# Differential attention: key and value projections of the next head issued in two runs of 12 matmuls, spread over all eight slots

## What is computed

```python
def diff_mixer(h, cos, sin, layer_idx, w_qkv, lam_q1, lam_k1, lam_q2, lam_k2, w_o):
    q, k, v = jnp.split(h @ w_qkv, [DIFF_QK_WIDTH, 2 * DIFF_QK_WIDTH], axis=-1)
    ...
    q = jnp.concatenate([apply_rope(q[..., :DIFF_ROPE], cos, sin), q[..., DIFF_ROPE:]], axis=-1)
    k = jnp.concatenate([apply_rope(k[..., :DIFF_ROPE], cos, sin), k[..., DIFF_ROPE:]], axis=-1)
    ...
        sc = jnp.einsum('bqhcd,bkhcd->bhcqk', qb, k).astype(f32) * scale
        p = jax.nn.softmax(sc, axis=-1)
        a = (p[:, :, 0] - lam * p[:, :, 1]).astype(v.dtype)
        return jnp.einsum('bhqk,bkhe->bqhe', a, v)
```

## Time and profile before

| | us |
|---|---|
| median of 3 runs | 3125.02 |
| lowest, highest | 3124.98, 3127.79 |
| span of the profiled execution | 3121.7 |
| TensorE busy in it | 2930.5 |
| VectorE busy | 1643.0 |
| ScalarE busy | 1230.4 |
| GpSimd busy | 1077.3 |

### The profile page before, as it was taken

One profiled execution on the slowest core, in us unless ns is written; L12 is line 12 of the kernel. 1 busy time (PEld: TensorE's weight loads), 2 busy tenths in 40 slices (PEclk: granted clock), 3 DMA queues, 4 the chain that ended last, 5 costly groups with the idle time before them and its releaser, 6 DMA issues. The chain is left out here.

```text
span 3121.7 us, 39393 instructions
## 1 busy us (share of the span) xinstructions
PE 2930.5 (94%) x14436; PEld 2442.1 (78%) x14436; DVE 1643.0 (53%) x2222; ACT 1230.4 (39%) x1830; POOL 1077.3 (35%) x807
## 2 busy tenths in 40 slices
PE   6799999999899999999978999998798999999997
PEld 5688888887688888888757887877777888888885
DVE  6477777773443333433457777777534333433335
ACT  4467666662322222212245565555313222212221
POOL 3333444332332233322244444443223233222330
PEclk9999999999999999999989999999899999999998
DMA  3000000002111111111020000000311111111111
GB/s 110 22 10 9 13 8 8 8 15 101 48 54 41 41 56 58 47 40 41 27 96 24 32 28 28 28 25 24 128 41 54 41 63 52 47 40 40 40 54 54
DMA packets 35816, 132.46 MB, mean 42 GB/s; under 512 B 4480, under 2 KB 4736, under 8 KB 35328
## 3 DMA queue, kind: packets, MB, share of 16 engines
q1 hardware_dynamic: 35712, 131.03, 12.0%
HBM read 117.38 MB, written 13.63 MB: 42 GB/s over the span
## 5 line engine op out<-in xcount | busy, mean ns | idle before, releaser
L320 POOL TENSOR_TENSOR weights_lo<-weights_raw,weights_hi 128x1024 fp32r<-128x1024 f32 (+1 forms) x150 | 356.7, 2378 | 1101.5 <-ACT weights_hi L315 1101.5
L329 PE MATMUL ffn_pre<-hh,weights_hi 128*128 128x512 f32 x1408 | 558.0, 396 | 11.0 <-POOL hl L170 9.4
L331 PE MATMUL ffn_pre<-hh,weights_lo 128*128 128x512 f32 x1408 | 556.9, 395 | 0.0
L330 PE MATMUL ffn_pre<-hl,weights_hi 128*128 128x512 f32 x1408 | 556.8, 395 | 0.0
L700 DVE SCALAR_TENSOR_TENSOR ffn_conv<-ffn_pre,vecs,ffn_conv 128x1023 f32<-128x1023 f32 x88 | 112.9, 1283 | 708.0 <-ACT ffn_conv L629 708.0
L629 ACT ACTIVATE ffn_conv<-ffn_pre,vecs 128x1024 f32<-128x1024 f32 x88 | 106.3, 1208 | 819.1 <-PE ffn_pre L331 819.1
L329 PEld LDWEIGHTS ffn_pre<-hh,weights_hi 128*128 128x128 f32 x1408 | 266.0, 189 | 77.5 <-issue 12.0
L331 PEld LDWEIGHTS ffn_pre<-hh,weights_lo 128*128 128x128 f32 x1408 | 266.1, 189 | 62.3
L330 PEld LDWEIGHTS ffn_pre<-hl,weights_hi 128*128 128x128 f32 x1408 | 266.1, 189 | 61.6
L329 PE MATMUL ffn_acc<-ffn_yh,ffn_dn_hi 128*128 128x512 f32 x704 | 275.6, 391 | 12.5 <-POOL ffn_dn_lo L320 12.5
L330 PE MATMUL ffn_acc<-ffn_yl,ffn_dn_hi 128*128 128x512 f32 x704 | 275.3, 391 | 0.0
(11 more groups left out here) (248 smaller groups left out, 6266.4 us busy)
## 6 DMA issues: line engine op xcount, KB each, us to landing
weights_raw<-in_up SPq DMA_DIRECT2D x88, 512.0 KB, 3.7
ffn_dn_raw<-in_down SPq DMA_DIRECT2D x44, 512.0 KB, 3.6
weights_raw<-in_diff_qkv SPq DMA_DIRECT2D x24, 512.0 KB, 3.7
weights_raw<-in_mla_heads SPq DMA_DIRECT2D x16, 320.0 KB, 2.8
heads<-in_x SPq DMA_DIRECT2D x8, 512.0 KB, 7.0
weights_raw<-in_mla_o SPq DMA_DIRECT2D x8, 512.0 KB, 3.9
x_first<-in_x SPq DMA_DIRECT2D x1, 4096.0 KB, 12.1
x_spill<-x_first SPq DMA_DIRECT2D x1, 4096.0 KB, 13.5
```

The costliest lines, as they stand in the source:

```text
L320: pool.tensor_tensor(w.lo[:], w.raw[:], w.hi[:].bitcast(F32), ALU.subtract).then_inc(w.lo_done, 1)
L329: pe.matmul(out, w_hi, x_hi, start=start, stop=False)
L330: pe.matmul(out, w_hi, x_lo, start=False, stop=False)
L331: return pe.matmul(out, w_lo, x_hi, start=False, stop=stop)
```

## The change

The number of instructions stays; their order within the queues of four engines changes.

- TensorE: `project` takes a range of its eight k-tiles. `begin` issues the first four (12 matmuls; it waits for the weight and for the bank), `complete` the last four (it signals `proj_ready`). K0 begins at t = 1 and is completed at t = 2, K1 at 2 and 3, V0 at 5 and 6, V1 at 6 and 7; a completion stands right behind the scores of its slot. At t = 3 the values come ahead of `turn_v(TURN0)`.
- ScalarE: K0, K1, V0 and V1 are taken at t = 2, 3, 6 and 7, right behind the exponentials.
- GpSimd: the cosine products of K0 and K1 move from t = 1 and 2 to t = 2 and 3, at t = 2 behind `low_q(Q1)`.
- VectorE: at t = 2 and 3 the shuffle comes behind the reciprocal; `low_v(TURN1)` moves from t = 4 to the end of t = 3.

```diff
@@ ScalarE, slot
+                if scores and more and t in (2, 3, 6, 7):
+                    take(h + 1, {2: K0, 3: K1, 6: V0, 7: V1}[t])
                 if t % 2 == 1 and not (first and t < LAG_V):
...
                     if t == 1:
                         split_high(act, wq, h + 1, bank(h, Q1) + 1)
-                        take(h + 1, K0)
-                    if t == 2:
-                        take(h + 1, K1)
...
-                    if t == 5:
-                        take(h + 1, V0)
                     if t == 6:
                         high_parts(h + 1, 1 - parity, Q0)
-                        take(h + 1, V1)
@@ GpSimd, slot
                     if t == 1:
                         split_low(pool, wq, h + 1)
+                    if t == 2:
                         by_cosine(h + 1, K0)
-                    if t == 2:
+                    if t == 3:
                         by_cosine(h + 1, K1)
-                    if t == 3:
                         split_low(pool, wkv, 2 * h + 3)
@@ VectorE, slot
-                    if turning:
+                    if turning and t not in (2, 3):
                         shuffle(*turning)
-                    if t == 4:
-                        low_v(h, TURN1)
-                        if more:
-                            rotate(h + 1, K1)
+                    if more and t == 4:
+                        rotate(h + 1, K1)
                     col = 2 * (t % 2)
                     dve.wait_ge(exp_done, 2 * n + 2)
                     dve.reciprocal(inv_sum[:, col:col + 2], row_sum[:, col:col + 2]).then_inc(inv_ready, 1)
+                    if turning and t in (2, 3):
+                        shuffle(*turning)
                     if t == 3:
                         low_v(h, TURN0)
...
+                if t == 3:
+                    low_v(h, TURN1)
                 if turning and t != 3:
                     rotate(*turning)
@@ TensorE
-            def project(h, use, w, content):
+            def project(h, use, w, content, rows=range(KT)):
...
-                wait_weight(pe, w, content)
-                need(pe, proj_taken, bank(h, use))
-                for k in range(KT):
+                if rows[0] == 0:
+                    wait_weight(pe, w, content)
+                    need(pe, proj_taken, bank(h, use))
+                for k in rows:
...
-                mm.then_inc(proj_ready, 1)
+                if rows[-1] == KT - 1:
+                    mm.then_inc(proj_ready, 1)
+
+            def begin(h, use, w, content):
+                project(h, use, w, content, range(KT // 2))
+
+            def complete(h, use, w, content):
+                project(h, use, w, content, range(KT // 2, KT))
...
+                if scores and more and t in (2, 3):
+                    complete(h + 1, K0 if t == 2 else K1, wkv, 2 * h + 2)
+                if scores and more and t in (6, 7):
+                    complete(h + 1, V0 if t == 6 else V1, wkv, 2 * h + 3)
+                if t % 2 == 1 and not (first and t < LAG_V):
+                    values(h, t)
                 if scores and t == 3:
                     turn_v(h, TURN0)
-                if t % 2 == 1 and not (first and t < LAG_V):
-                    values(h, t)
...
                     if t in (1, 2):
-                        project(h + 1, K0 if t == 1 else K1, wkv, 2 * h + 2)
+                        begin(h + 1, K0 if t == 1 else K1, wkv, 2 * h + 2)
...
                     if t in (5, 6):
-                        project(h + 1, V0 if t == 5 else V1, wkv, 2 * h + 3)
+                        begin(h + 1, V0 if t == 5 else V1, wkv, 2 * h + 3)
```

## The result

| | median, us | profiled execution, us |
|---|---|---|
| kernel before, same session | 3125.0 | 3121.7 |
| changed kernel | 3181.8 (3175.6 to 3183.7) | 3173.4 |

The ratio is 1.0178, with a 95% interval of 1.0163 to 1.0192: slower by 56.8 us. The forecast was 3190, within 3165 to 3212.

What follows compares the result with a forecast made beforehand. TensorE sets the pace, with a four-engine loop per slot close behind. A head: 9.0 - 1.3 + 1.85 = +9.6 us; seven heads 67, less 2, total +65, so the median becomes 3190, range 3165 to 3212.

Steps and rivals of the forecast that it cites:

- Step 2: Slot 2: K1's second half waits for ScalarE's copy of K0, late behind both exponentials; 2.3 us lost a head.
- Step 3: Slots 2 and 3: K0's cosine product behind low_q delays rotation, mix and maxima; TensorE waits 6.1 us before TURN0 every head.
- Item 4: Slots 2 and 3: VectorE's one-column add and shuffle, now behind the reciprocal, held by GpSimd's scaling; 1.2 us, bounds 0 and 2.5.
- the -2 below: Correction over all heads: old TURN waits swallowed by the new wait, first head lacking values; -2 us, between -6 and +2.
- Item 5: Slot 3: lower clock after the 6.1 us wait slows TURN0 and T(3); 0.3 us on the chain, 0 to 0.8.
- Step 7: Slots 5 to 7: late mix for slot 6 delays V1's first half; S(5) to next S(0) 27.15, today 25.30: +1.85 us.
- step 1: TensorE's slots by itself; T(0) keeps its wait for the mix, only S(0) lying between T(7) and T(0); cost 0.
- The rival "faster": No exponential late, projection halves run on arrival, waits of 1.52 and 1.70 go: 28 us, so 3097; chance 0.02.
- The rival at 3140: The rotation's wait does not bite, low_q being done before K0's product is wanted; +2 a head; chance 0.07.

Runs made afterwards that it cites:

- e5: e1 with GpSimd's split of wq in slot 1 waiting until VectorE has finished Q1's rotation; 3124.7 us, ratio 1.0004 to the kernel before.
- e1: Changed kernel with GpSimd's cosine product of K0 moved ahead of low_q in slot 2; 3139.8 us, ratio 1.0047 to the kernel before.
- e2: Changed kernel with VectorE's rotation of K0 moved behind the maxima of slot 3, GpSimd's order kept; 3141.1 us, ratio 1.0046 to the kernel before.
- e8: e7 with V1's second half behind the transposes of slot 7 and ScalarE's copy of V1 at that slot's end; 3101.4 us, ratio 0.9930.
- e7: e5 with VectorE's low part of K1 moved from the end of slot 5 to the end of slot 6; 3113.5 us, ratio 0.9969.
- e10: Kernel before, whole projections, with the edits of e5 and e7; 3146.7 us, ratio 1.0074.

## Why the prediction was right

Its sign and mechanism held, and most terms are within a few tenths. Counted from S(1) = 1791.93:

- Step 2. Mix for slot 2 at 10.67 (10.66 forecast), K1 at 16.03 (16.1), S(3) at 18.94 (18.95). Shown by e5.
- Step 3. low_q starts at 19.45 (19.55), its end and the product 0.1 and more earlier: product 25.1 to 26.4 (25.2 to 26.5), mix 27.02 (27.15), TURN0 32.39 (32.65), TensorE's wait 5.77 (6.1; 5.3 in the mean of seven heads). e1 and e2 show that this queue is three quarters of the loss.
- Item 4 was mis-sized: 1.2 us a head forecast, none measured. In slot 2 the one-column add was indeed held (0.95), off the path; in slot 3, started 0.07 after the scaling had begun, it took 0.19. The row from which I took the price was an add of 512 columns beside a long split. Seven times 1.2 is 8.4 us, and the forecast was too high by as much (3190 for 3182), but that is chance: the next items take a part of it back, and the -2 below was too small.
- Item 5. TURN0 to its high part took 1.16 and to TURN1 2.62 in all, where 2.02 is the figure at the higher level: 0.6 more and not 0.3. From TURN1 to S(4) it took 0.71 where 0.41 was counted, so that the clock cost 0.9 on this chain, above the stated 0 to 0.8. The granted clock of the 15 us around it was 0.78, and 0.50, the level of 1.2 GHz, from 1824.0 to 1829.5, behind the wait of 5.8.
- S(4) came at 35.72 (36.55), Q0 3.91 after it (3.7); V1 waits 1.50 (1.93), and S(5) to the next S(0) takes 26.87 (27.15). The head is 83.54, 8.7 above the 74.83 of before; 9.6 were forecast.
- Step 7 rests on a wrong reading. The prediction gave head 3 of the kernel before the length of head 2 (74.83) and so its slot 7 the length 5.73. The next score matmul is at 1922.63, so head 3 lasts 76.43 and its slot 7 7.33. In head 2, S(5) to the next S(0) took 25.17, close to the 25.30 that the prediction used, so this did little harm.
- The seven heads. Head 2 alone would make 7 x 8.7 = 61. The seven heads together lost 55.2, because heads 0, 1 and 6 lost only 7 each: in the kernel before, slots 3 and 4 of these heads had the longer waits that the new one swallows. The prediction put this at -2; it measured -6, the end of its range. For the phase it forecast 65 and 55 were measured; the median rose by 57, so the sum is 10 too high in the profile and 8 in the median.
- The wait before T(0) stayed (step 1; 1.06 in head 2), and e8 shows its reason: 2.83 us of matmuls between T(7) and T(0) remove it.
- From the first score matmul of head 0 to that of head 7 the changed kernel takes 581.5 us (1617.69 to 2199.18) and the kernel before 526.3 (1620.71 to 2147.03): 55 us, so the loss is in this phase. The span grew by 51.7, since the phase began 3.0 earlier in the changed kernel's profile.
- The rival "faster" named two conditions that mattered but were not enough. With K0's product ahead of low_q (e1) and the mix for slot 2 at 8.66 after S(1) (e5; 8.3 was asked), the time was 3125, that of the kernel before. It took the edits of e7 and e8 as well to come to 3101, and e8's gain is the wait before T(0), which the rival's 3097 did not contain, so that the two figures are near is partly luck. The rival at 3140 is what e1 measured: it is the change without this one queue.

## What to carry to other kernels

When work is moved in an in-order queue, look at what stands behind each instruction that waits for it, on every engine: the product stood at 25.1 after S(1) instead of the 17.1 of e1, for a rotation that had time (e2), and the mix behind the rotation had none. When the bottleneck engine's slots are evened out, chains that a long slot had hidden come to the surface; count every chain again against the new slot lengths before judging the idea, and mend those first. A wait can shorten a chain: of two operations that hold each other up, let the one that nobody waits for start second (e5).

## What the runs showed of the hardware

In the pairs that these traces show, a VectorE operation with two SBUF inputs and a GpSimd operation take turns, and the one that starts second is stretched by about what is left of the first: the add took 2.70 beside GpSimd's split and 0.69 ahead of it (2.0 more, with 2.2 of the split left; e5), the mix 3.37 and 1.28 (e10), GpSimd's split 3.29 behind a mix (e5) and 2.35 where it started first (e10). This agrees with the Trainium skill (GPSIMD Engine Reference, Key points), which names the contention without a size. What I had not expected: a split that started 0.06 us ahead of the mix made the mix pay (e10).

A one-column add started 0.07 after a GpSimd scaling had begun slipped in (0.19), while one started 0.25 after was held to its end (0.95). This is no single case: in every profile in which the add stands behind the reciprocal, those started 0.02 to 0.08 after the scaling took 0.16 to 0.20 (heads 0, 1 and 6 of the changed kernel have this in slot 2 too), and those started 0.24 to 0.26 after took 0.95 or 0.96. Beside GpSimd's cosine product, which has two inputs, an add started 0.01 after it was held for 1.27 (heads 0, 1 and 6 of the kernel before). Why the first was let in, no run here tells.
